# Transposed growth of triangle inverses in four quadrants, five attention units weighted on GpSimd, shorter fillers, another closing order

## The reference

```
h = x
for layer in range(2):
    u = rms_norm(h, norm_mix[layer])
    if layer == 0:
        cols = u @ hyb_w_in
        mix = concat([rwkv7_mix(cols[..., :RWKV_COLS]), nsa_mix(cols[..., RWKV_COLS:])]) @ hyb_w_out
    else:
        mix = mamba2_mix(u)
    h = h + mix
    h = h + hier_moe(rms_norm(h, norm_ffn[layer]))   # 4 groups x 8 experts, top 2 of one group
return rms_norm(h, norm_final)
```

## Time and profile before

| | us |
|---|---|
| median of 3 runs (lowest, highest) | 1313.13 (1312.91, 1313.23) |
| the profiled execution | 1313.46 |
| its span in the profile | 1311.7 |
| TensorE busy | 1217.1 |
| VectorE busy | 401.3 |
| ScalarE busy | 270.5 |
| GpSimd busy | 43.8 |
| read from HBM | 460.54 MB, 352 GB/s over the span |

### The profile page before, as it was taken

One profiled execution on the slowest core, in us unless ns is written; L12 is line 12 of the kernel. 1 busy time (PEld: TensorE's weight loads), 2 busy tenths in 40 slices (PEclk: granted clock), 3 DMA queues, 4 the chain that ended last, 5 costly groups with the idle time before them and its releaser, 6 DMA issues.

```text
span 1311.7 us, 20829 instructions
## 1 busy us (share of the span) xinstructions
PE 1217.1 (93%) x8760; PEld 668.8 (51%) x8760; DVE 401.3 (31%) x1016; ACT 270.5 (21%) x556; POOL 43.8 (3%) x35
## 2 busy tenths in 40 slices
PE   9999999999998888698999999999999997887987
PEld 5778755444443333353588886454444443333432
DVE  1287846121111110111257655152121112101111
ACT  2344523101010000010224665031101110000102
POOL 1003200000000000000000110000000000000000
PEclk9999999999999998798999999999999999897989
DMA  7633499999999999999944475979999999999996
GB/s 278 204 112 124 139 353 390 427 428 427 425 429 428 427 426 428 424 426 425 354 170 160 161 288 206 372 307 427 426 428 426 428 427 426 428 426 425 428 426 261
DMA packets 55754, 463.10 MB, mean 353 GB/s; under 512 B 8608, under 2 KB 9920, under 8 KB 26464
## 3 DMA queue, kind: packets, MB, share of 16 engines
q1 hardware_dynamic: 55504, 461.57, 85.9%
q10 hardware_dynamic: 144, 0.07, 0.0%
HBM read 460.54 MB, written 1.08 MB: 352 GB/s over the span
## 4 chain that ended last, share of the span: by engine, by line
PE 67%; DMA 24%; DVE 4%; issue 2%; ACT 2%; another core or an unknown queue 1%; DVEq 0%; SPq 0%; ACTq 0%
DMA raw<-in_moe_w_up 17%; PE bank L2243 10%; DMA raw<-in_moe_w_gate 7%; PE bank L2224 6%; PE sums L2938 6%; PE sums L2290 5%; PE bank L2180 5%; PE bank L3079 4%; PE bank L2281 4%; PE bank L2938 4%; PE bank L2268 3%; PE bank L1245 3%; PE bank L2254 2%; PE bank L1277 2%; PE bank L1709 1%
## 5 line engine op out<-in xcount | busy, mean ns | idle before, releaser
L2243 PE MATMUL bank<-raw,xg 128*32 128x512 f32 x1664 | 233.4, 653 | 47.8 <-DMA raw<-in_moe_w_up 42.4
L2153 DVE TENSOR_TENSOR aT<-bank,sg 128x128 f32<-128x128 f32 (+1 forms) x64 | 20.3, 317 | 551.0 <-ACT sg L2048 551.0
L2243 PEld LDWEIGHTS bank<-raw,xg 128*32 128x32 f32 x1664 | 57.7, 118 | 197.9 <-issue 122.4
L2180 PE MATMUL bank<-sel,ux 128*128 128x64 f32 (+1 forms) x896 | 117.7, 287 | 16.2 <-DVE sel L2070 15.3
L2180 PEld LDWEIGHTS bank<-sel,ux 128*128 128x128 f32 x896 | 110.9, 202 | 39.9 <-issue 21.6
L2290 PE MATMUL sums<-ys,selT 64*128 64x512 f32 x512 | 127.2, 615 | 1.6 <-DVE ys L2166 1.6
L2045 ACT COPY gus<-bank 128x512 f32<-128x512 f32 x64 | 37.5, 585 | 437.6 <-PE bank L2243 332.5
L2281 PE MATMUL bank<-raw,aT 128*32 128x512 f32 x832 | 100.0, 598 | 9.4 <-DVE aT L2153 9.4
L2290 PEld LDWEIGHTS sums<-ys,selT 64*128 64x128 f32 x512 | 44.1, 186 | 84.5 <-issue 80.3
L2938 PE MATMUL sums<-uT,wr 128*128 128x256 f32 x384 | 85.6, 381 | 0.0
L2224 PE MATMUL bank<-raw,xg 128*64 128x512 f32 x384 | 84.7, 594 | 0.0
(11 more groups left out here) (443 smaller groups left out, 1247.0 us busy)
## 6 DMA issues: line engine op xcount, KB each, us to landing
raw<-in_moe_w_gate SPq DMA_DIRECT2D x54, 2048.0 KB, 40.0
raw<-in_moe_w_up SPq DMA_DIRECT2D x54, 2048.0 KB, 44.4
raw<-in_moe_w_down SPq DMA_DIRECT2D x54, 2048.0 KB, 43.9
raw<-in_moe_w_gate SPq DMA_DIRECT2D x20, 1024.0 KB, 11.1
raw<-in_moe_w_up SPq DMA_DIRECT2D x20, 1024.0 KB, 10.7
raw<-in_moe_w_down SPq DMA_DIRECT2D x20, 1024.0 KB, 10.5
wr<-in_ssm_w_in SPq DMA_DIRECT2D x10, 2048.0 KB, 8.0
odd<-in_hyb_w_in SPq DMA_DIRECT2D x2, 2048.0 KB, 10.5
```

The costliest lines, as they stand in the source:

```text
L2180: i = T.matmul(bank[SIDE_BANK][:, k * n:(k + 1) * n].rearrange("p (x s) -> p x s", x=2), ux[:, t, 4 * half + k, :], src[:, t, :, :], start ...
L2243: i = T.matmul(bank[GU_BANK][CAP_S * c:CAP_S * c + CAP_S, :], xg_f[:, x, 4 * half + k, :], raw[:, slot, k * FH:(k + 1) * FH], start=(half ...
```

## The change

It does four things. TensorE issues dTT for both groups at once with `crossed, straight`; group 1's result then lies in swapped halves, and VectorE adds it as two instructions of 64 partitions that read one half and write the other. Of units 3 to 7, VectorE does only the reciprocal and the gate (`shares(i)`), between the reads of dT and of dTT of the level (unit 7: after the copies of wu), and GpSimd does the multiplication; in GpSimd's order masked(4) moves ahead of weighted(3) and of the multiplication by the gate. `idle()` issues three matmuls of 128 columns instead of two of 256. In the final norm VectorE weights half 0 of tile 1 ahead of the inverse of tile 0.

```diff
-        def weighted(i):
+        def shares(i):
             t, br, g = UNITS[i]
-            w = P * (t + 1)
             dve.wait_ge(*at("exp", i))
             did(V.reciprocal(den[:, i, :], den[:, i, :]))
             did(V.tensor_tensor(den[:, i, :].rearrange("p (e m) -> p e m", e=2),
                                 den[:, i, :].rearrange("p (e m) -> p e m", e=2),
-                                gv[:, t, g * GQ:(g + 1) * GQ, br + 1].rearrange("p (m e) -> p e m", e=2), ALU.mult))
+                                gv[:, t, g * GQ:(g + 1) * GQ, br + 1].rearrange("p (m e) -> p e m", e=2), ALU.mult),
+                "shares", i)
+        def weighted(i):
+            w = P * (UNITS[i][0] + 1)
+            shares(i)
             go(V.tensor_tensor(pr[:, i % 2, :, 0:w], pr[:, i % 2, :, 0:w], rep(den[:, i, :], w, 2), ALU.mult),
                "weighted", i)
...
-        def grown(l):
+        def grown(l, unit=None):
             for name, dst in (("dT", tri), ("dTT", triT)):
+                if name == "dTT" and unit is not None:
+                    shares(unit)
                 if name == "dT" and l == LAST:
                     continue
                 for g in range(2):
                     dve.wait_ge(*at(name, l, g))
                     sl = dst[:, HEADS * g:HEADS * g + HEADS, :]
-                    go(V.tensor_tensor(sl, bank_of(name, l, g)[:, :].rearrange("p (c s) -> p c s", s=CHK), sl,
-                                       ALU.add), "read", name, l, g)
+                    grew = bank_of(name, l, g)[:, :].rearrange("p (c s) -> p c s", s=CHK)
+                    if name == "dTT" and g:
+                        for q in range(2):
+                            go(V.tensor_tensor(sl[at64(1 - q)], grew[at64(q)], sl[at64(1 - q)], ALU.add),
+                               *(("read", name, l, g) if q else ()))
+                    else:
+                        go(V.tensor_tensor(sl, grew, sl, ALU.add), "read", name, l, g)
...
         scores(3)
-        grown(2)
-        weighted(3)
+        grown(2, 3)
         scores(4)
         compressed_turned(1)
-        grown(3)
-        weighted(4)
+        grown(3, 4)
         scores(5)
-        grown(4)
-        weighted(5)
+        grown(4, 5)
         scores(6)
-        grown(5)
-        weighted(6)
+        grown(5, 6)
         scores(7)
...
-        weighted(7)
+        shares(7)
...
         masked(3)
+        def weighted(i):
+            w = P * (UNITS[i][0] + 1)
+            pool.wait_ge(*at("shares", i))
+            go(G.tensor_tensor(pr[:, i % 2, :, 0:w], pr[:, i % 2, :, 0:w], rep(den[:, i, :], w, 2), ALU.mult),
+               "weighted", i)
+        masked(4)
+        weighted(3)
         pool.wait_ge(*at("read", "gup", 1))
         pool.wait_ge(pool_done, PO.n)
         go(G.tensor_tensor(pre, pre, gate[:, :, :], ALU.mult))
-        masked(4)
+        weighted(4)
         pool.wait_ge(pool_done, PO.n)
         go(G.tensor_tensor(gate[:, :, :], gate[:, :, :], rep(gn_w, HALVES), ALU.mult), "gain")
+        weighted(5)
         router_weighted(pool, 0)
+        weighted(6)
+        weighted(7)
...
-            for g in range(2):
-                squares({g: take(pe, "dTT", l, g, pool=right)}, prod, triT, crossed, crossed).then_inc(
-                    pe_done, PE.one(("dTT", l, g)))
+            bs = {g: take(pe, "dTT", l, g, pool=right) for g in range(2)}
+            squares(bs, prod, triT, crossed, straight).then_inc(pe_done, PE.one(("dTT", l, 1)))
+            new[("dTT", l, 0)] = new[("dTT", l, 1)]
...
             def idle():
-                for _ in range(2):
-                    T.matmul(bank[SIDE_BANK][:, 0:2 * P], C("ident"), cst[:, 0:2 * P], start=True, stop=True)
+                for _ in range(3):
+                    T.matmul(bank[SIDE_BANK][:, 0:P], C("ident"), cst[:, 0:P], start=True, stop=True)
...
             sums_weighted(dve, "final", o_f, 0, 1)
+            sums_weighted(dve, "final", o_f, 1, 0)
             inverse(dve, "final", 0, std_f, rstd_f)
             nc.vector.tensor_scalar(o_f[:, 0, :], o_f[:, 0, :], rstd_f[:, 0:1], None, ALU.mult).then_inc(
                 dve_done, DV.one(("scaled", 0)))
             sums_part(dve, "final", 1, ss_f, ss_f[:, 2 * HALVES:])
-            sums_weighted(dve, "final", o_f, 1, 0)
             inverse(dve, "final", 1, std_f, rstd_f)
```

## The result

The kernel after takes 1324.42 us (median of 4 runs, 1322.73 to 1325.84), the one before 1313.02 in the runs beside it: 11.4 us or 0.85% more, ratio 1.0085 with a 95% interval of 1.0072 to 1.0098. The forecast was 1314.4 with a range up to 1317.8. The profiled execution took 1325.84 us (before: 1313.46), its span 1324.1. Medians in this document are of the runs in the fast state; one run of the kernel before (3057.62 us) and one of experiment 4 (1747.69 us) are outside it.

The account below looks back on a forecast made before the run. TensorE and VectorE, both nearly full, were taken to bound the hybrid stage, the weight stream the experts. 1313.46 + 3.2 (stage) - 0.85 (fillers) - 1.05 (closing order) = 1314.8, less 0.33: 1314.4 us; range 1311.0 to 1317.8.

Parts of the forecast that it names:

- the replay: Hybrid stage: engine queues carried forward from 118.4 us with usual durations and waits; stage 3.2 us longer.
- Levels 1 and 2: Hybrid stage: dTT ends 0.98 us earlier, but weights_turned(2) waits for VectorE's extra 0.6, leaving only 0.13.
- rival 1: Ahead of weights_turned(3): the clock falls in the new 3.6 us gap, costing 1.7 more, 1316.1 us; chance 0.25.
- TensorE's part: Hybrid stage: dTT in four corners takes 0.98 us instead of 2.04, saving 4.9 us over five levels.
- VectorE's part: Hybrid stage: additions of 64 partitions cost no less than 128, so 0.6 us more per level, 3.0 together.
- The quadrants alone: Hybrid stage: four-corner dTT and its split additions, weighting left on VectorE, make the stage 1.0 us longer.
- Prices on GpSimd: Weighting of units 3 to 7: 1.9 us for 128x1024 and 1.05 for 128x512; upper end 2.83 and 1.4.
- The order on GpSimd: Unit 3: masked(4) ahead of weighted(3) makes TensorE stand still 3.6 us before weights_turned(3).
- The loop: Hybrid stage after unit 3: shares, dTT additions, scores, maximum and exponentials set a pace of 7.06 us per level.
- weighted(7): End of hybrid stage: on GpSimd it ends at 168.4, weights_turned(7) wants it at 169.3; hidden, 0.9 us to spare.
- Rival 2: Unit 3: the stall is not paid; stage at -0.4 us, time 1310.8 us; chance 0.13.
- The fillers: Both closings: three matmuls of 128 columns instead of two of 256 save 0.43 us per closing, 0.85 for two.

Follow-up runs that it names:

- experiment 4: Changed kernel with 12 and 11 identity products on TensorE ahead of its waits for units 2 and 3: 1323.09 us, ratio 1.0077.
- experiment 5: Changed kernel with GpSimd held back until weighted(2) before it adds gn_b: 1318.82 us, ratio 1.0038.
- experiment 9: Kernel before with only dTT in four corners and its three additions, GpSimd also waiting for weighted(2) before adding gn_b: 1319.82 us, ratio 1.0063.
- experiment 12: Kernel before with VectorE copies and products on an unused tile, put where GpSimd begins two long products: a 128x128 copy took 2.41 us, not 0.23.
- swapped kernel: Changed kernel with only weighted(3) put ahead of masked(4) on GpSimd: 1318.31 us, ratio 1.0056.
- held and swapped: Changed kernel with GpSimd waiting for weighted(2) before adding gn_b, and weighted(3) ahead of masked(4): 1312.08 us, ratio 0.9997.
- experiment 10: Kernel before with only four-corner dTT and its three additions, GpSimd waiting for weighted(2) before gn_b and weighted(3) before masked(4): 1316.57 us, ratio 1.0025.
- Experiment 3: Changed kernel with old dTT, fillers and final order, leaving only the weighting on GpSimd with masked(4) ahead: 1318.28 us, ratio 1.0036.
- experiment 1: Kernel before with only the shorter fillers and the new order of the final norm: 1310.98 us, ratio 0.999.
- experiment 8: Held and swapped, plus 4 identity products on TensorE ahead of its wait for weighted(5): 1311.26 us, ratio 0.9985.

## Why the prediction was wrong

It was too low by 10 us. Slower had a chance of 0.31 in it, but the time lies beyond its range, and none of its rivals explains it alone.

**The step that failed** is the one in the replay: "Levels 1 and 2: dTT ends 0.98 earlier, but weights_turned(2) waits for VectorE, which has 0.6 more to do: only 0.13 is left." It let each engine take its usual time whatever the others did. VectorE and GpSimd do not: where both read two SBUF operands, the second to start waits until the other's instruction has ended (VectorE 1.99 us instead of 0.17, GpSimd 2.83 instead of 2.35). The rows were there: the 2.83 us of line 994 in the earlier trace rows, which I took as the upper end of a price ("others of 1024 elements go from 2.40 to 2.83") where it was the 2.35 us of the work and 0.48 of waiting. Experiments 5, 9 and 12 show the wait itself. In its place the meeting cost 4.0 us at unit 2. The Trainium skill has the rule (SBUF — State Buffer, SBUF: two separate sides): VectorE with two SBUF inputs, or in a two-port mode, and GpSimd share a pair of ports, and whichever starts first keeps it for its whole instruction. The traces agree: 1.99 us for 128x4 elements behind a GpSimd instruction, 2.83 for 2.35 the other way round, and 2.41 for 0.23 for the float32 copy of experiment 12. By that rule the forecast would have been an estimated 1318.4, the 1314.4 and 4.0 us more at unit 2, taken one to one.

A second term stood at nothing in the sum: the clock, which only rival 1 had, with one fall of 1.7 us. In the account below three falls take 7.1 us.

**Where the time went.** At the end of wu the change is 14.4 us late (159.92 to 174.36):
- 3.2 us forecast;
- 4.0 us the meeting: weights_turned(2) at 130.38 instead of 126.34;
- 3.1 us the clock behind that gap: the products with the compressed values, kt, dT with dTT and scores take 1.43, 1.90, 3.62 and 1.23 us of the chain instead of some 1.00, 1.02, 1.97 and 1.06;
- 1.5 us the clock behind the forecast gap;
- 2.5 us the clock ahead of wu: from weights_turned(6) to the mark 6.92 us, in the swapped kernel, with no fall there, 4.41;
- 0.3 us for weights_turned(6) in two pieces, the 4.41 against 4.10 before.

The two rows of the swapped kernel:

```profile
163.17 0.66 PE L1276 MATMUL bank<-cst,pr 128*128 128x128 f32 x4 [1.68 <-POOL pr L1009]
...
167.58 1.13 PE L1691 MATMUL bank<-zz,qk 128*128 128x512 f32 x2
```

That is 14.6, 0.2 too much. Of the 14.4, the first load that waits for the stage still has 14.0, the start of the last closing 13.84; there the fillers take 0.45 and the order 1.0, and 12.4 remain between the two profiled executions. The after one is the slowest of its four runs; the medians are 11.4 apart. The sum is worked out from rows of single executions, and no experiment measures one of its terms alone; experiments 5 to 7 bear it as a whole: held and swapped takes back 13.8 us of the mark.

Point by point:
- **TensorE's part** held: 64 records of dTT in 1.11 to 1.16 us instead of 2.04. **VectorE's part** was sized too small: 64 partitions cost no less than 128, as forecast, but the two of 64x512 take 1.41 us, and the three additions of the level 2.13 (123.14 to 125.27) where the two of before take 1.33. That is 0.8 us more per level and not 0.6. "The quadrants alone +1.0" measured 14.3, and 3.0 without the meetings. The warning of the Trainium skill that I cited there (TensorEngine Tiling (Array Packing), Performance Considerations: tiling speeds TensorE, not the reading of PSUM) is borne out: in experiment 10 TensorE gains 0.9 us per level and waits 0.94 to 1.49 us for VectorE.
- **Prices on GpSimd** held to 0.01: 1.04 and 1.89 us for 1.05 and 1.9. **The order on GpSimd** held: 3.52 us for 3.6. Experiment 3, which has only this part, lies at 1318.28, within what was expected of it (1317 to 1319.5).
- **The loop**, 7.06 us per level: shares at 150.45, 157.71, 164.97, so 7.26; the 0.2 is that of VectorE's additions. **weighted(7)** hidden: yes.
- **Rival 1, the clock**, was right, but I let it happen once; it fell behind both long gaps and once more. A forecast of 1316.1 would still have missed, as the meeting makes the second gap. Nor does the length of a gap alone tell whether the clock falls: it fell behind 1.66 us in the kernel after and behind 1.00 in the held and swapped one, and stayed at 1.00 behind 1.68 in the swapped one.
- **Rival 2**, no stall, is refuted by the 3.52. Its number, the replay of the swapped order with -0.4, holds only with the meeting away: the swapped kernel has the mark 7.7 us late.
- **The fillers**: 0.46 us in layer 0's closing as forecast (0.43), but by the start of the last closing it was given back (13.85 us late ahead of layer 0's closing, 13.39 behind it, 13.84 at the end of layer 1's stream). In the trace of experiment 1 it was kept (0.96 us early ahead of layer 0's closing, 1.41 behind it, 1.86 ahead of the last). So whether the fillers give half of the 0.85 or all of it, one execution of each kernel doesn't tell. The order gave 1.0 us in both (forecast 1.05). The root of the last tile, 1307.11 before, stands after at

```profile
1319.50 0.29 ACT L244 ACTIVATE std_f<-ss_f 128x1 f32<-128x1 f32 x1
```

  that is 12.39 us later, 13.84 less the fillers' 0.45 and the order's 1.0.
- **The range** missed as it was made of the bounds of prices and of one fall of the clock; no bound stood for two engines that delay each other.

**What stays open.** Why the clock falls ahead of wu in the kernel after (gap of 1.66 us), in that of experiment 4 (1.66) and in the held one (1.67), but not in the swapped one (1.68). What came earlier may count; or it differs from execution to execution of one kernel, as times and mean clocks do (experiment 5: 1316.20 us at 0.970, 1321.57 at 0.963). With one trace of each kernel no run here tells. The same doubt hangs over the single falls in experiments 8 and 10.

## What to carry to other kernels

Before moving an instruction by half a microsecond, look for VectorE instructions of two SBUF operands that begin within a few tenths of a GpSimd instruction: there the first to start makes the other wait for its whole length, and a row in the trace of before that is longer than its like (2.83 for 2.35, 0.32 for 0.17) shows that the two already touch. Where they do, let GpSimd wait for VectorE's short instruction: one wait was worth 5.6 us here. And a long gap on TensorE costs more than its length: between 120 and 160 us, in all these kernels, TensorE passed to the lower clock behind every gap of 3.26 us or more. What that costs depends on what waits behind them; in experiment 8, where it was GpSimd's weighting, a fall of the clock cost nothing at the mark.

## What was not expected of the hardware

- VectorE's product of 128x4 took 1.92 to 2.19 us beside a GpSimd instruction, 0.17 alone; a float32 copy 128x128 in SBUF took 2.41 instead of 0.23.
- GpSimd's 128x1024 with one operand repeated along the innermost dimension takes 1.89 us, VectorE's 1.23; with plain operands, or one repeated over rows, GpSimd takes 2.34 to 2.40.
- The granted clock went down behind gaps of 3.3 to 4.1 us in each kernel that had one in this stage (to 0.50 over 4 us in the held kernel), but also behind gaps of 1.0 and 0.27 in a stretch of 64x64 products (0.57 from 150 to 154 us in the held and swapped kernel), while a gap of 1.40 in the held kernel and the 3.14 us of the earlier trace rows passed without.
